# Another order of the first loads and of one weight load in a two-layer encoder kernel

## The reference, cut to what matters

```python
h = x                                             # (1, 512, 1024)
# layer 0: convolution mixer
hn = rmsnorm(h, norm_mix[0])
u = hn @ w1 + b1;  a, gate = split(u)             # w1 is 1024 x 2048
u = a * sigmoid(gate)
u = depthwise_conv_31_taps(u) + b_dw              # causal, along the sequence
h = h + silu(layernorm(u)) @ w2 + b2
h = h + relu(rmsnorm(h) @ mlp_w1[0]) ** 2 @ mlp_w2[0]    # 1024 -> 4096 -> 1024
# layer 1: pooling mixer
hn = rmsnorm(h, norm_mix[1])
p = [trailing_mean(hn[:, g], width) - hn[:, g]  for the 4 channel groups g, width in (2, 4, 8, 16)]
h = h + (p @ pool_w + pool_b) * pool_scale        # four 256 x 256 maps
h = h + relu(rmsnorm(h) @ mlp_w1[1]) ** 2 @ mlp_w2[1]
out = rmsnorm(h, final_norm)
```

## Time and profile before

| | |
|---|---|
| median of 3 runs | 931.42 us (928.91 to 932.8) |
| the profiled execution | 930.72 us, its span 928.9 us |
| PE busy | 894.4 us, 96% of the span |
| DVE busy | 694.0 us, 75% |
| ACT busy | 452.7 us, 49% |
| POOL busy | 144.1 us, 16% |
| all DMAs | 90.84 MB, mean 98 GB/s |

### The profile page before, as it was taken

How to read it: one execution, slowest core, us unless ns; L and a number is a source line. 1 busy time by engine, 2 the same in 40 slices (tenths; PEclk the granted TensorE clock), 3 DMA queues, 4 the chain that set the end, 5 groups by cost and what they waited for, 6 DMA issues and landing times.

```text
span 928.9 us, 11872 instructions
## 1 busy us (share of the span) xinstructions
PE 894.4 (96%) x4423; PEld 757.3 (82%) x4423; DVE 694.0 (75%) x923; ACT 452.7 (49%) x655; POOL 144.1 (16%) x121
## 2 busy tenths in 40 slices
PE   6999988999999999999999969999999999999996
PEld 5888876789888888888888859988888888888885
DVE  5799999867468778686868676846868768686865
ACT  4787685345253726344373343543452726345342
POOL 0499982057000000000000121000000000000000
PEclk9999999999999999999999979999999999999999
DMA  9514013115123131423311320313223131423102
GB/s 302 158 46 114 19 72 114 65 72 190 65 109 136 46 135 45 152 93 117 136 45 68 103 102 23 112 70 126 87 106 135 45 135 45 156 95 111 68 1 90
DMA packets 48377, 90.84 MB, mean 98 GB/s; under 512 B 1458, under 2 KB 18866, under 8 KB 48340
## 3 DMA queue, kind: packets, MB, share of 16 engines
q1 hardware_dynamic: 48340, 90.32, 27.7%
HBM read 88.22 MB, written 2.10 MB: 97 GB/s over the span
## 4 chain that ended last, share of the span: by engine, by line
PE 78%; DVE 8%; POOL 7%; ACT 2%; DMA 2%; issue 1%; SPq 0%; DVEq 0%; POOLq 0%; ACTq 0%
PE ps L1197 17%; PE ps L1199 17%; PE ps L1198 17%; PE ps L1371 8%; PE ps L1373 8%; PE ps L1372 8%; POOL merged_a L363 3%; POOL w_lo L353 2%; DVE ps L825 2%; POOL merged_b L363 2%; PE ps L1234 1%; DMA w_raw<-in_mlp_w 1%; DMA h<-in_x 1%; PE ps L1214 1%; DVE w_lo L933 1%
## 5 line engine op out<-in xcount | busy, mean ns | idle before, releaser
L1197 PE MATMUL ps<-act_hi,w_hi 128*128 128x512 f32 (+1 forms) x720 | 265.3, 368 | 3.1 <-DVE act_lo L760 3.1
L1199 PE MATMUL ps<-act_hi,w_lo 128*128 128x512 f32 (+1 forms) x720 | 263.9, 367 | 0.0
L1198 PE MATMUL ps<-act_lo,w_hi 128*128 128x512 f32 (+1 forms) x720 | 263.8, 366 | 0.0
L1197 PEld LDWEIGHTS ps<-act_hi,w_hi 128*128 128x128 f32 x720 | 136.5, 190 | 25.6 <-DVE act_lo L760 4.0
L581 ACT ACTIVATE relu<-ps 128x512 f32<-128x512 f32 x40 | 23.9, 598 | 269.5 <-PE ps L1199 268.2
L1199 PEld LDWEIGHTS ps<-act_hi,w_lo 128*128 128x128 f32 x720 | 136.6, 190 | 22.1
L1198 PEld LDWEIGHTS ps<-act_lo,w_hi 128*128 128x128 f32 x720 | 136.5, 190 | 21.6
L1371 PE MATMUL ps<-w_hi,u_hi 128*128 128x512 f32 x336 | 130.7, 389 | 0.0
L1372 PE MATMUL ps<-w_lo,u_hi 128*128 128x512 f32 x336 | 130.7, 389 | 0.0
L1373 PE MATMUL ps<-w_hi,u_lo 128*128 128x512 f32 x336 | 130.7, 389 | 0.0
L978 DVE TENSOR_TENSOR w_lo<-w_raw,w_hi 128x1024 fp32r<-128x1024 f32 x60 | 73.3, 1221 | 66.4 <-ACT w_hi L607 66.4
(11 more groups left out here) (183 smaller groups left out, 1344.9 us busy)
## 6 DMA issues: line engine op xcount, KB each, us to landing
w_raw<-in_mlp_w SPq DMA_DIRECT2D x32, 1024.0 KB, 4.9
w_raw<-in_mlp_w SPq DMA_DIRECT2D x16, 2048.0 KB, 8.0
w_raw<-in_conv_w SPq DMA_DIRECT2D x16, 512.0 KB, 5.4
w_raw<-in_conv_w SPq DMA_DIRECT2D x2, 2048.0 KB, 9.1
h<-in_x SPq DMA_DIRECT2D x4, 512.0 KB, 6.6
out<-tok SPq DMA_DIRECT2D x8, 256.0 KB, 2.0
gain<-in_norm_mix SPq DMA_DIRECT2D x2, 512.0 KB, 6.0
gain<-in_norm_mlp SPq DMA_DIRECT2D x2, 512.0 KB, 6.0
```

The costliest lines, as they stand in the source:

```text
L1197: nc.tensor.matmul(dst, lh, rh, start=(n == 0), stop=False)
L1198: nc.tensor.matmul(dst, lh, rl, start=False, stop=False)
L1199: return nc.tensor.matmul(dst, ll, rh, start=False, stop=(n == count - 1))
```

## The change

There are two parts. In the second, at the start of layer 1, SP issues the 2 MB load of the first group's first weights ahead of the wait for `pw_lo_ok` and the load of the pooling bias that stands behind this wait. In the first, at the head, SP issues both first blocks of `x`, then the gain row, the two weight halves, the other two blocks, and the four parameter loads behind them; the two halves have a semaphore each; ACT, DVE and PE have their lists arranged to fit, with the parameters' transpose behind pair 0 and their copy behind the last `act_low`.

```diff
         cw_in = [sem(f"cw_in{k}") for k in range(2)]
+        cw_first_in = [sem(f"cw_first_in{k}") for k in range(2)]
...
-                                 ).then_inc(cw_in[s], 16)
+                                 ).then_inc(cw_in[s] if e else cw_first_in[a], 16)
...
-            for b in range(NB):
+            def load_x(b):
                 sp.dma_start(h[:, b, :], x[0, b * P:(b + 1) * P, :]).then_inc(x_in[b], 16)
-                if b == 0:
-                    sp.dma_start(gain[:, 0, :], row(norm_mix[0])).then_inc(gain_in[0], 16)
-                if b == 1:
-                    sp.dma_start(par_rows[0:16], conv_dw[0, 0:16]).then_inc(par_in, 16)
...
-                    load_cw(0, 0)
+
+            load_x(0)
+            load_x(1)
+            sp.dma_start(gain[:, 0, :], row(norm_mix[0])).then_inc(gain_in[0], 16)
+            load_cw(0, 0)
+            load_x(2)
+            load_x(3)
+            sp.dma_start(par_rows[0:16], conv_dw[0, 0:16]).then_inc(par_in, 16)
...
             load_cw(1, 1)
...
             sp.dma_start(gain[:, 0, :], row(norm_mix[1])).then_inc(gain_in[0], 16)
+            sp.wait_ge(w1_lo_ok, 4 * GROUPS)
+            load_m1(1, 0)
             sp.wait_ge(pw_lo_ok, 1)
             sp.dma_start(tok[:, 1, :], pool_b[0].rearrange("g d -> (g d)").rearrange("(o d) -> o d", o=1)
                          .to_broadcast([P, D])).then_inc(pb_in, 16)
-            sp.wait_ge(w1_lo_ok, 4 * GROUPS)
-            load_m1(1, 0)
             sp.wait_ge(w2_lo_ok, LAYER_SPLITS)
...
-                act.wait_ge(cw_in[s], 32 * k + 32)
+                act.wait_ge(cw_in[s], 32 * k + (32 if s else 0))
...
             def cw_high_half(a, done):
+                act.wait_ge(cw_first_in[a], 16)
                 nc.scalar.copy(cw_hi[:, 0, :, a, :], cw_raw[:, 0, :, a, :]).then_inc(done, 1)
...
+            x_root(0)
+            x_root(1)
+            cw_high_half(0, cw_half_hi)
+            act_high(GEN_X, 0)
+            act_high(GEN_X, 1)
+            cw_high_half(1, cw_hi_ok)
+            x_root(2)
+            x_root(3)
+            act_high(GEN_X, 2)
+            act_high(GEN_X, 3)
             cw_high(0, 1)
...
+            x_norm(0)
+            x_norm(1)
+            cw_low_half(0, cw_half_hi, cw_half_lo)
+            act_low(GEN_X, 0)
+            act_low(GEN_X, 1)
+            cw_low_half(1, cw_hi_ok, cw_lo_ok)
+            x_norm(2)
+            x_norm(3)
             act_low(GEN_X, 2)
-
             act_low(GEN_X, 3)
+            dve.wait_ge(par_t, 1)
+            nc.vector.tensor_copy(params[:, :, 0:NPAR],
+                                  ps[:, 2, 0:NC * NPAR].rearrange("p (c k) -> p c k", c=NC)).then_inc(par_ok, 1)
             cw_low(1, 1)
...
             keep_clock(12)
-            param_turn()
             turn(GEN_X, 1, tok[:, 1, :])
...
+                if pair == 0:
+                    param_turn()
             last.then_inc(glu_mm, 1)
```

More of the change, by code:

```diff
@@ L274, in _ @@
             c2_src = conv_w2[0].rearrange("(c p) d -> p c d", p=P)
-            for b in range(NB):
+            def load_x(b):
                 sp.dma_start(h[:, b, :], x[0, b * P:(b + 1) * P, :]).then_inc(x_in[b], 16)
-                if b == 0:
-                    sp.dma_start(gain[:, 0, :], row(norm_mix[0])).then_inc(gain_in[0], 16)
-                if b == 1:
-                    sp.dma_start(par_rows[0:16], conv_dw[0, 0:16]).then_inc(par_in, 16)
-                    sp.dma_start(par_rows[16:TAPS], conv_dw[0, 16:TAPS]).then_inc(par_in, 16)
-                    sp.dma_start(par_rows[TAPS:TAPS + 1], conv_dwb).then_inc(par_in, 16)
-                    sp.dma_start(par_rows[TAPS + 1:TAPS + 3],
-                                 conv_b1[0].rearrange("(a d) -> a d", a=2)).then_inc(par_in, 16)
-                    load_cw(0, 0)
+            load_x(0)
[5 more added lines that the diff above has]
+            sp.dma_start(par_rows[0:16], conv_dw[0, 0:16]).then_inc(par_in, 16)
+            sp.dma_start(par_rows[16:TAPS], conv_dw[0, 16:TAPS]).then_inc(par_in, 16)
+            sp.dma_start(par_rows[TAPS:TAPS + 1], conv_dwb).then_inc(par_in, 16)
+            sp.dma_start(par_rows[TAPS + 1:TAPS + 3], conv_b1[0].rearrange("(a d) -> a d", a=2)).then_inc(par_in, 16)
             load_cw(1, 1)
@@ L444, in _, with x_root @@
             nc.scalar.activation(stats[:, 3, 38:39], stats[:, 4, 38:39], ACT.Sqrt)
-            for b in range(NB):
+            def x_root(b):
                 act.wait_ge(x_in[b], 16)
                 square(NORM_X, b, ctok[:, 2, :])
-                if b == 2:
-                    act_high(GEN_X, 1)
-                    cw_high_half(1, cw_hi_ok)
                 root(NORM_X, b)
-                if b in (1, 3):
-                    act_high(GEN_X, b - 1)
-                if b == 1:
-                    act.wait_ge(cw_in[0], 32)
-                    cw_high_half(0, cw_half_hi)
-            act_high(GEN_X, NB - 1)
+            x_root(0)
[8 more added lines that the diff above has]
+            act_high(GEN_X, 3)
             cw_high(0, 1)
@@ L773, in _, with x_norm @@
             nc.vector.memset(stats[:, 4, 38:39], 1.0).then_inc(stats_ok, 1)
-            for b in range(NB):
+            def x_norm(b):
                 rms(NORM_X, b, False)
@@ L781, in _ @@
                 normed(NORM_X, b, tok[:, b % 2, :], tok_ok)
-                if b == 1:
-                    act_low(GEN_X, 0)
-                    dve.wait_ge(par_t, 1)
-                    nc.vector.tensor_copy(params[:, :, 0:NPAR],
-                                          ps[:, 2, 0:NC * NPAR].rearrange("p (c k) -> p c k", c=NC)).then_inc(par_ok, 1)
-                    cw_low_half(0, cw_half_hi, cw_half_lo)
-                    act_low(GEN_X, 1)
-                    cw_low_half(1, cw_hi_ok, cw_lo_ok)
+            x_norm(0)
[6 more added lines that the diff above has]
+            x_norm(3)
             act_low(GEN_X, 2)
             act_low(GEN_X, 3)
+            dve.wait_ge(par_t, 1)
+            nc.vector.tensor_copy(params[:, :, 0:NPAR],
+                                  ps[:, 2, 0:NC * NPAR].rearrange("p (c k) -> p c k", c=NC)).then_inc(par_ok, 1)
             cw_low(1, 1)
```

## The result

| | before | after |
|---|---|---|
| median | 930.56 us (928.91 to 935.12, 7 runs) | 919.0 us (918.22 to 924.17, 7 runs) |
| the profiled execution | 930.72 us, span 928.9 | 922.61 us, span 920.6 |
| PE busy | 894.4 us | 892.6 us |

The ratio of after to before is 0.9886, with a 95% interval of 0.9856 to 0.9916: faster by 1.1%, some 10.6 us. Six more runs of the same kernel in a later series had a median of 920.57 (ratio 0.9895, 0.9873 to 0.9917); the middle one of all 13 is 920.29. After's seven runs lie in two heaps, 918.2 to 919.0 with a mean granted clock of 0.996 to 0.997, and 922.6 to 924.2 with 0.990 to 0.992; the six later ones don't part so clearly (918.2, three from 919.98 to 920.85, 922.46 and 923.97). The profiled execution is one of the second heap, which matters for what follows.

A forecast was written before the change was run, and what follows sets the result against it. PE's work bounds the kernel (busy 894.4 of 928.9 us), plus its waits and low clock. 930.72 - 10.75 (layer 1) - 1.0 (head) = 918.97, or 919.7 from the median; put at 919.2, range 915.8 to 923.5.

The forecast's parts named there:

- The load and its cover: Start of layer 1: 2 MB load issued near 496.5, there by 506; DVE's 1.2 us split free, add 0 at 531.4.
- The pause: PE ahead of `pool_turn(0)`: wait falls from 7.59 us to about 1.1, start at 539.9 for 546.41, gaining 6.5 us.
- The clock under tiles 6 and 7: PE from `pool_turn(0)` through tiles 6 and 7: 7.2 us for 11.05, gaining 3.85 if the clock stays up.
- rival of the short pause: Ahead of `pool_turn(0)`: the clock falls in the 1.1 us pause too, losing the 3.85; 922.8 us, chance 0.12.
- DVE as the next bound: Pooling mixer: DVE and ACT, slack 5.2 us against 5.35 needed, are next to be late; 0.2 taken off.
- rival 1: Pooling mixer: DVE and ACT can't follow, PE gets only the pause's 6.5 us; 923.2 us, chance 0.12.
- The second fall: Clock behind `pool_turn(1)`: 1.5 us returns only without this fall; part gives 11.5 without it, 10.0 with, middle 10.75.
- sign that I gave for `mlp_up_first(1)`: First product of layer 1's MLP: starts 10 to 12.8 us earlier than 585.45, the head's share included.
- The head: Start of the kernel, block 1 second and gain third in the queue: 1.0 us gain, ends of 2.0 and -0.5.
- the one on the fillers and the gain row ahead of them: Head: gain at 8.2 to 8.7, 12 fillers of 2.31 us, block 1's transpose at 12.9 to 13.9, products 16.3 to 17.5.
- a pass at full clock at 19 to 20: Head, PE: clock was at half there; full clock helps only if `normed(2)` is ready, which it isn't; no gain counted.
- The layer 1 part: Early 2 MB load at layer 1's start: 10.75 us gain, from 11.5 with the clock up throughout and 10.0 with a fall.

The follow-up runs named there:

- filled pause: Kernel before with 33 extra matmuls of 128x512 into an unused bank ahead of `pool_turn(0)`, results unread: 926.48 us, ratio 0.9948.
- the same kernel with 12 fillers: Kernel after with the gain row second and tile 7 and products 0 and 1 laid into the first halves of the pool turns: 918.04 us, ratio 0.9851.
- mixed list: PE's order in five kernels built on after, with matmuls of tile 7 and products 0 and 1 laid between `pool_turn` steps: medians 917.92 to 920.16 us.
- gain second: Kernel after with the gain row back in second place of the queue, between the two blocks of `x`: 919.11 us, ratio 0.9868.
- 2 fillers: Kernel after with 2 fillers in place of 12 ahead of the transpose of block 1: 920.44 us, ratio 0.9889.
- mixed early: Kernel after with matmuls of tile 7 and products 0 and 1 laid into the first half of each of `pool_turn(1)` to `(3)`: 919.38 us, ratio 0.9871.
- load alone: Kernel before with only layer 1's 2 MB load and its wait moved ahead of the `pw_lo_ok` wait and the bias: 921.43 us, ratio 0.9883.
- load late: Kernel before with the 2 MB load ahead of the bias load, both behind the wait for `pw_lo_ok`: 927.41 us, ratio 0.9961.
- mixed version: Kernel after with half of tile 7 and of products 0 and 1 laid between the steps of `pool_turn(1)`, `(2)` and `(3)`: 920.16 us, ratio 0.988.

## Why the prediction was right, and where it was not

The forecast was 919.2; the median is 919.0, and 920.29 over all 13 runs. By its steps:

- **The load and its cover.** Issue at 496.5 (measured 496.55), the bias in its place, the split of the first part free, add 0 at 531.4 (531.46). Right.
- **The pause.** `pool_turn(0)` at 539.9 (539.99), the pause 1.1 (1.09), a gain of 6.5 (6.50; 6.42 between the two starts, since PE ended tile 5 0.08 later). Right.
- **The clock under tiles 6 and 7.** 3.85 forecast, 3.67 in the trace, 3.83 in that of the kernel with the filled pause and about 4.0 by its times. Right. What the rival of the short pause foresaw, a clock that falls there, was in one of ten traces with the early load; there `pool_turn(1)` was reached 7.60 us behind `pool_turn(0)` against 6.15 in the trace of the same kernel with 12 fillers, so the fall cost 1.45 and not 3.85, and the whole mixer took 35.44 us in place of 34.75.
- **DVE as the next bound.** The wait for `act_high(2)` shrank from 4.41 to 1.06, and the add at 570.25 waits 1.77 for PE. DVE didn't take the gain away; rival 1 falls.
- **The second fall.** The step that was mis-sized. I allowed for one later fall, as in the trace of before, or none, and took the middle of 10.0 and 11.5. The traces of kernels with the old list in the mixer have one or two; those with the mixed list have none there (but for the early one above). The mixer's length goes by that count: with two falls 37.21 (after), 37.17 (its repeat) and 37.18 (the filled pause); with one 35.65 (gain second) and 35.62 (2 fillers); with none 34.75 (mixed early, whose own order costs something too). The load alone had a second fall that lasted from 565.7 to 572.5 and took 38.72. The forecast for one was 39.04 - 3.5 = 35.54, and for none 34.04. The price of a fall, 1.5, was right for all but that long one; the number of them I took from one trace. With the fall near 145 us, of which the prediction says nothing and which costs 1.0, it would account for most of the 4.4 us between after's heaps: 1.0 + 1.5 + 1.5. So the part gave 8.25 + 0.08 = 8.3 us in the profiled execution (0.08 for the later end of tile 5), and 39.04 - 35.65 + 6.42 = 9.8 in one with one fall, in place of 10.75. By this the sign that I gave for `mlp_up_first(1)`, 10 to 12.8 us earlier than 585.45, failed in the profiled execution (8.25) and held in the repeat (10.6). The low stretch of before that I put at 9.6 us at most is 10.2 by the earlier trace rows, from 544.0 to 554.3, which changes nothing in the sum.
- **The head.** Forecast 1.0, measured nothing that can be told from zero, and 0.1 in the mean of the gates. The failed step is the one on the fillers and the gain row ahead of them. The gain row (8.33), the transpose of block 0 (9.67) and `normed(1)` (10.85) came in the ranges given; but the 12 fillers took 2.77 in place of 2.31 and the transpose of block 1 started at 14.00, above the 13.9 of the slow end, and took 1.81. I had put the products at 16.3 to 17.5; they came at 18.16, and at 16.87, 17.15, 17.47 and 17.69 in the other traces of this head, so the slow end was the normal case. The two experiments on it name both parts: the gain in third place costs the wait at `normed(0)` (1.04 to 2.29 us in six traces), and the fillers come out of the shade. Taking either away moves the gate by 1.5 and 2.6 against the first trace of after, and by 0.8 and 1.9 against the mean of five; taking both away moves it no further, since then block 1 is third. The parameters' late load and transpose cost nothing visible (0.68 us ahead of pair 1).

  One reading in the prediction was wrong besides: that a pass at full clock at 19 to 20 would help only if `normed(2)` were ready, "which it isn't". In before's trace it was ready at 21.04, and PE came to the transpose of block 2 at 21.93, without a wait. In the traces of the same head without the fall (load alone, load late) PE waits for it, and the gate is at 32.94 and 32.88 in place of 33.76. So the fall behind the pause of 1.89 us cost the head about 0.8 in the trace that I summed against. The row of `normed(2)` before, and the transpose of block 2 with the load alone:

```profile
19.76 1.28 DVE L754 SCALAR_TENSOR_TENSOR tok<-h,rinv,gain 128x1024 f32<-128x1024 f32 x1
```

```profile
20.85 1.09 PE L1214 MATMUL ps<-ident,tok 128*128 128x128 f32 x8 [0.52 <-DVE tok L754]
```

- **The sum.** The layer 1 part was too high by 0.9 to 2.4 us by the traces (the medians of the load alone give it 10.0 us) and the head by about 1; that the median of the first seven still came out at 919.0 is in part luck. Four of the seven were of the first heap, with one fall at most, and one of the six later ones; over all 13 it is 920.29. In part it is the base: the executions of before have the same kind of scatter (928.91 to 935.12), and its profiled one is not its best.

The Trainium skill, "TensorE: Matmul & The Clock Gate", section "HAM oscillation — how this bites in real kernels", explains a clock that falls in DMA waits between bursts. For the 7.59 us pause, which goes back to the late 2 MB load, the traces agree (0.52 within it from 544 on, 0.50 behind it, and 1.00 with the pause filled). The later falls are not of that kind: PE was busy for all but 0.99 of the 12 us from 539 to 551, and this 0.99 is the pause that ends at 539.99. The section states nothing of such a case.

What stays open: why a fall comes behind a `pool_turn` in one execution and not in another of the same kernel, and whether it is the small shape of its matmuls. The mixed version had a clock of 0.998 in five of five runs; it changes the shapes and the order at once, and its trace also lacks the fall near 145 us, which has nothing to do with the mixing.

## What to carry to other kernels

Look at what a wait on the DMA queue holds back: a load whose own buffer had been free for 30 us stood behind a wait for something else, and moving it cut a 7.6 us pause on the matrix engine to 1.1 and gave some 3.7 us of clock besides. When a transfer is given a better place at the head, price the one that loses it: here one row in third place held up the chain by 1.0 to 2.3 us, and fillers that had been in the shade of a wait came into the path. If an engine's speed can change within a run, count such changes in several executions before pricing them from one trace.

## What the runs showed of the hardware that I had not expected

- The granted clock fell while PE was fully busy. The last matmuls of `pool_turn(1)` in after (32 matmuls, of 128x128 and 128x16, without a gap from 547.37 on) and the first of the product, behind a gap of 0.17 us, in order of time:

```profile
550.67 0.22 PE L1449 MATMUL ps<-band_prev,w_hi 128*128 128x16 f32 x1
550.75 0.26 PE L1451 MATMUL ps<-band_prev,w_lo 128*128 128x16 f32 x1
551.17 0.35 PE L1206 MATMUL ps<-pw_hi,act_hi 128*128 128x256 f32 x1 [0.17 <-DVE h L963]
551.36 0.33 PE L1207 MATMUL ps<-pw_lo,act_hi 128*128 128x256 f32 x1
551.49 0.41 PE L1208 MATMUL ps<-pw_hi,act_lo 128*128 128x256 f32 x1
```

  From 551.49 on the product's matmuls stand 0.21 apart, until the clock is back. The second fall has no gap ahead of it; it came within `pool_turn(3)`:

```profile
565.00 0.27 PE L1451 MATMUL ps<-band_prev,w_lo 128*128 128x16 f32 x1
565.12 0.45 PE L1446 MATMUL ps<-band,w_hi 128*128 128x128 f32 x1
```

  With larger matmuls between the small ones the clock stayed at 1.00 at both places in the traces of all five kernels that have them.
- The clock also fell at or behind short pauses, and not each time: behind that of 2.4 us near 145 in ten of fourteen traces, behind that of 1.1 to 1.9 at the head before the first product in two of four (at 1.77 and 1.89, not at 1.15 and 1.67), behind that of 1.09 ahead of `pool_turn(0)` in one of ten. Behind those of 5.46, 7.59 and 7.90 it was down each time.
- At the head the same transpose has two prices. In after the 12 fillers at 11.44 take 0.23 us each and the 16 at 15.64 0.12 each, while the granted clock reads 1.00 over both; in another trace 16 fillers took 3.54. The prediction called this half clock; the record of the clock doesn't show it, so what it is stays open.
- The same 2 MB load took 9.28 us behind the bias's issue and 7.48 ahead of it; the bias took 4.3 from issue to landing as the first, no more than where the load is away (3.4 to 4.6), and 8.5 as the second. So of two transfers issued together the one behind pays: 1.8 us for the load, 4.2 for the bias.
